# Making k from rows that the first norm has not scaled yet, in a two-block kernel on one core

## The chip, the cores and the metric

The kernel runs on one core of a Trainium2 chip. The time is the device time of one execution in microseconds, and the number given is the median of three executions. All arithmetic is float32.

## The reference, cut to what matters

Two transformer-like blocks are computed on 512 tokens of width 1024, with 16 meta tokens put in front (528 rows in all). The change touches only the start of the first block:

```python
def rmsnorm(x, g):
    ms = mean(x * x, axis=-1)                     # one number for each row (token)
    return x * rsqrt(ms + EPS) * g                # g: one number for each channel
xn = rmsnorm(concat(meta_tokens, x), g_mix_pre)
proj = xn @ w_in                                  # 1024 x 6160
q, k, v, r, a_low, u, z_gla, z_ssm = split(proj)
log_a = log_sigmoid(a_low @ w_gate_up + b_gate) / 16
o = gla_chunked(q, k, v, log_a)                   # causal gated linear attention, chunks of 64
...
```

What follows (the SSM branch, GLU, feed-forward, and the second block with attention, convolution and a mixture of experts) is the same before and after.

The factor rsqrt(ms + EPS) belongs to a token and the product with `w_in` runs over channels, so that (x g s) W = s ((x g) W) for the scale s of each token.

## The kernel before, in words

Everything is kept with channels on the partitions and tokens along the free dimension: x is the tile `x_in` (`HT0`), 8 blocks of 128 channels by 528 tokens. Weights come in 1 MB units of 128x2048 float32 in the order of a list (`PLAN`: k 0 and 1, v 0 to 3, q 0 and 1, u, r and so on). A unit lands in one of three `ring` buffers. ScalarE copies it to a rounded high part (`high`, line 936), VectorE subtracts to get the low part (`low`, lines 1532 to 1536), both into one of two sides of `wsplit`, and TensorE makes three products of each pair (high by high, high by low, low by high; `three`). Unit n can be split only when unit n-2 has been used, and a ring buffer is loaded again when its low part is made.

Each engine has its own function (`tensor`, `scalar`, `vector`, `gpsimd`, `sync`), whose instructions run in the order in which they are written; names in a table stand for semaphore counts (`sig` sets one, `at` waits for one). PSUM's eight banks go round: `fresh` takes the bank that was closed longest ago and waits until its last tenant was read out ("free"). All 8 banks have had the eight `gate` products of line 458 as tenants when unit v 2 starts, so its first bank is free when VectorE has read the first of them at line 1698.

The start of the program, engine by engine:

- SyncE issues the loads of `vecs`, `cst`, x in four pieces, `wal`, `wgu`, three weight units, `bc`.
- ScalarE squares the 8 blocks of x (line 969), TensorE sums the squares over channels with a matrix of ones (lines 418 to 424: 8 products of 512 and 8 of 16 columns), ScalarE takes the root (line 962), VectorE the reciprocal (1548). The result `rstd` (`rst`) holds each token's scale on every partition.
- VectorE makes x g s block by block (1563, 128x528), ScalarE its high part (976), and VectorE (even blocks, 1567) and GpSimd (odd blocks, 2480) the low part. `at("xn", k)` is block k.
- TensorE makes k: unit k 0 block by block as xn comes, four banks at once (`linear` with `each`), 96 products of 264 columns, then unit k 1, 96 more, then the 48 small products of the low gate (`alow`, line 431), then v 0 and v 1, 60 products of 512 columns each, then the `gate` products (458), which need `alow_out` of VectorE (1575), then v 2 and so on.
- ScalarE copies k out of PSUM (950) and takes part in a chain of small operations on SSM parameters.
- VectorE does that chain behind the norm: lines 1657 to 1690, with `next_low` for k 1 (at 1662), v 0 (at 1682) and v 1 (at 1688) between its parts, then four `turns` (1621), `next_low` for v 2, `alow_out`, two `weights_out` (1638), and then the 8 additions of line 1698 that read the gate banks. All of this is in one fixed order.

Of the kernel before, what the change touches and what calls it, by code (L numbers as in the profile page):

```python
# [16 lines left out]
NT = 528  # L17
# [130 lines left out]
def program(nc, W, wmoe, mcst, vecs, cst, xT, wal, wgu, bc, rw, posr, posc, xslot, yslot, prep, bbar, ushuf, yshuf, out):  # L148
    ctx = ExitStack()
    with ctx:  # L150
# [60 lines left out]
        def vec(name):  # L211
            o, n = VOFF[name]
            return vt[:, o:o + n]
# [8 lines left out]
        HT0 = tile("x_in", 0, 8, NT)  # L222
# [40 lines left out]
        rt4 = small[:, 44:48]  # L263
# [93 lines left out]
        def tensor(g):  # L357
# [20 lines left out]
            def linear(name, i, cuts, nk=8, size=2048, each=None, beside=None, after=None):  # L378
# [23 lines left out]
                for j in range(per):  # L402
                    m = slice(128 * j, 128 * j + 128)
                    for tag, xh, xl in cuts:
# [7 lines left out]
                        banks.close(name, per * i + j, tag)  # L412

            halves = [(n, xnh[:, :, lo:hi], xnl[:, :, lo:hi]) for n, (lo, hi) in enumerate(HALVES)]
            xr = [(0, xnh[:, :, 16:NT], xnl[:, :, 16:NT])]

            ba, bb = fresh("ms", 0), fresh("ms", 1)
            p.wait_ge(cst_landed, 16)
            for k in range(8):  # L420
                p.wait_ge(*at("sq", k))
                mm(ba, ones, sq[:, k % 4, 0:512], k == 0, k == 7)
                mm(bb[:, 0:16], ones, sq[:, k % 4, 512:NT], k == 0, k == 7).then_inc(*p.sig(("ms", 0), ("ms", 1), ("summed", k)))
            banks.close("ms", 0)
            banks.close("ms", 1)

            for i in range(2):
                linear("k", i, halves, each="xn")
            for h, (lo, hi) in enumerate(HALVES):  # L430
                b = fresh("alow", h)[0:16, 0:hi - lo]
                p.wait_ge(*at("wal"))
                for k in range(8):
                    t = three(b, walh[:, k, :], wall[:, k, :], xnh[:, k, lo:hi], xnl[:, k, lo:hi], k == 0, k == 7)
                t.then_inc(*p.sig(("alow", h)))
                banks.close("alow", h)
# [492 lines left out]
        def scalar(g):  # L929
# [33 lines left out]

            for k in range(8):
                a.wait_ge(x_landed[k // 2], 16)
                if k > 3:
# [1840 lines left out]
```

## Time and profile before

| | us |
|---|---|
| median of three executions | 1802.95 (1801.0 to 1804.73) |
| the profiled execution | 1801.47 |
| its span in the trace | 1799.6 |
| TensorE busy | 1683.7 (94% of the span) |
| VectorE busy | 1208.6 (67%) |
| ScalarE busy | 748.4 (42%) |
| GpSimd busy | 306.6 (17%) |

The span runs from the first to the last instruction of the trace; the profiled execution's own time is 1.87 us longer. Times inside the trace are counted from the start of the span. A busy TensorE is one that has a matmul under way, not one at its peak. "Idle before" of an instruction is the time that its engine waited, with the instruction that released it.

### The profile page before, as it was taken

How to read it: one execution, taken by the hardware profiler on the slowest of the kernel's cores; microseconds unless marked ns; L12 is line 12 of the kernel's file. 1: busy time of each engine (PE TensorE's matmuls, PEld its weight loads, DVE VectorE, ACT ScalarE, POOL GpSimd, SP SyncE). 2: the span in 40 equal slices, each digit the busy share in tenths (PEclk: the TensorE clock that was granted, in tenths of full speed). 3: DMA queues.
4: the chain of work that ended last, by engine and by line, in shares of the span. 5: the costliest groups of instructions: out<-in, count | busy, mean ns of one | idle time of the engine just before them, and what ended most of it. 6: DMA issues, size and time to landing. Idle time of an engine off the chain costs nothing. (4 is left out here: it accounts for less than half of the span.)

```text
span 1799.6 us, 19630 instructions
## 1 busy us (share of the span) xinstructions
PE 1683.7 (94%) x8110; PEld 1324.5 (74%) x8110; DVE 1208.6 (67%) x1568; ACT 748.4 (42%) x969; POOL 306.6 (17%) x178
## 2 busy tenths in 40 slices
PE   6999899899999989999999989999898997999994
PEld 5778777677888867888887877878544776777773
DVE  5979768863333347733656446959787556999996
ACT  5252454444222333222222224342466136777773
POOL 1000012114000000000000015433200003554540
PEclk9999999899999989999999979999999999999997
DMA  5425222423222313435435412222200205999993
GB/s 233 165 102 180 77 95 67 138 88 129 111 94 94 140 71 140 164 117 210 164 116 187 164 48 77 94 94 94 71 0 1 94 1 201 395 386 390 368 376 146
DMA packets 59642, 264.52 MB, mean 147 GB/s; under 512 B 21648, under 2 KB 22288, under 8 KB 33056
## 3 DMA queue, kind: packets, MB, share of 16 engines
q1 hardware_dynamic: 34896, 159.10, 24.3%
q0 software_dynamic: 15184, 99.90, 14.1%
q10 hardware_dynamic: 9472, 4.26, 0.8%
q8 instruction: 64, 1.05, 0.2%
q14 instruction: 26, 0.21, 0.0%
HBM read 239.80 MB, written 23.44 MB: 146 GB/s over the span
## 5 line engine op out<-in xcount | busy, mean ns | idle before, releaser
L368 PE MATMUL bank<-h_high,wsplit 128*128 128x512 f32 x992 | 325.2, 405 | 11.5 <-ACT norm_tmp L1235 4.9
L1536 DVE TENSOR_TENSOR wsplit<-ring,wsplit 128x2048 fp32r<-128x2048 f32 x75 | 171.8, 2290 | 159.5 <-ACT wsplit L936 159.3
L936 ACT ACTIVATE wsplit<-ring 128x2048 fp32r<-128x2048 f32 x98 | 187.0, 1908 | 208.2 <-PE bank L368 197.0
L368 PEld LDWEIGHTS bank<-h_high,wsplit 128*128 128x128 f32 x992 | 188.8, 190 | 60.0 <-ACT norm_tmp L1235 5.0
L368 PE MATMUL bank<-xn_high,wsplit 128*128 128x512 f32 (+1 forms) x832 | 217.2, 348 | 12.1 <-DVE xn_low L1567 8.0
L368 PE MATMUL bank<-h_low,wsplit 128*128 128x512 f32 x496 | 198.0, 399 | 0.0
L368 PEld LDWEIGHTS bank<-xn_high,wsplit 128*128 128x128 f32 x832 | 145.5, 190 | 34.7 <-DVE xn_low L1567 8.1
L368 PE MATMUL bank<-f_high,wsplit 128*128 128x512 f32 x512 | 168.3, 401 | 0.0
L368 PE MATMUL bank<-xn_low,wsplit 128*128 128x512 f32 (+1 forms) x416 | 143.8, 346 | 0.0
L1536 POOL TENSOR_TENSOR wsplit<-ring,wsplit 128x2048 fp32r<-128x2048 f32 x23 | 106.8, 4643 | 176.5 <-ACT wsplit L936 176.4
L2561 POOL DMA_INDIRECT ring<-in_wmoe,indices x42 | 84.4, 2009 | 192.0 <-DVE routing L2328 131.5
L2528 POOL TENSOR_TENSOR x<-x,z 128x512 f32<-128x512 f32 x8 | 11.1, 1386 | 610.6 <-DVE z L2008 610.6
L368 PEld LDWEIGHTS bank<-f_high,wsplit 128*128 128x128 f32 x512 | 96.3, 188 | 22.0
L368 PEld LDWEIGHTS bank<-h_low,wsplit 128*128 128x128 f32 x496 | 94.6, 191 | 23.4 <-issue 1.8
L368 PE MATMUL bank<-f_low,wsplit 128*128 128x512 f32 x256 | 101.2, 395 | 0.0
L2123 DVE SCALAR_TENSOR_TENSOR bank<-conv_in,vecs,bank 128x512 f32<-128x512 f32 x116 | 87.7, 756 | 4.1
L368 PEld LDWEIGHTS bank<-xn_low,wsplit 128*128 128x128 f32 x416 | 79.0, 190 | 10.7 <-issue 1.0
L368 PE MATMUL bank<-m_high,wsplit 128*128 128x512 f32 x256 | 81.4, 396 | 3.8 <-DVE wsplit L1536 2.9
L368 PE MATMUL bank<-g_high,wsplit 128*128 128x512 f32 x256 | 80.8, 395 | 0.0
L368 PE MATMUL bank<-wsplit,block_high 128*128 128x512 f32 x232 | 75.5, 407 | 5.4 <-DVE block_low L2382 5.4
L1278 ACT ACTIVATE f_high<-norm_tmp 128x512 fp32r<-128x512 f32 x32 | 20.3, 634 | 122.0 <-DVE norm_tmp L2067 122.0
L368 PE MATMUL bank<-parts,block_high 128*128 128x512 f32 x216 | 68.9, 400 | 0.0
(480 smaller groups left out, 3337.3 us busy)
## 6 DMA issues: line engine op xcount, KB each, us to landing
ring<-in_W SPq DMA_DIRECT2D x122, 1024.0 KB, 4.8
weights_out<-prep SPq DMA_DIRECT2D x8, 864.0 KB, 5.6
prep<-weights_out_early POOLq DMA_DIRECT2D x8, 576.0 KB, 3.1
xslot<-zeros SPq DMA_DIRECT2D x7, 516.0 KB, 5.0
yslot<-block_out SPq DMA_DIRECT2D x7, 512.0 KB, 8.9
block<-xslot SPq DMA_DIRECT2D x6, 516.0 KB, 12.1
prep<-turns_early POOLq DMA_DIRECT2D x8, 288.0 KB, 2.4
x_in<-in_xT SPq DMA_DIRECT2D x4, 528.0 KB, 6.5
```

The source lines that it names most:

```text
L368: return g.matmul(o, l, r, start=first, stop=last_, skip_group_check=True)
L936: g.activation(wst[:, side(n), 0, :], ringt[:, n % RING, :], ACT.Copy).then_inc(*a.sig(("high", n)))
L1278: g.activation(fh[:, j % 16, :], nrm[:, 2 * z, :], ACT.Square).then_inc(*a.sig(("f_high", j)))
L1536: g.tensor_tensor(wst[:, side(n), 1, :], ringt[:, n % RING, :], hi, SUB).then_inc(*t.sig(("low", n), ("released", n)))
L2123: g.scalar_tensor_tensor(out=o, in0=i, scalar=cw[:, c, k:k + 1], in1=grown, op0=MUL, op1=ADD).then_inc(*v.sig(("convolved",), ("free", "co ...
L2528: g.tensor_tensor(X[:, k, :], X[:, k, :], Z[:, k, :], ADD).then_inc(*q.sig((name, "x", k)))
L2561: g.indirect_dma_start(slots[c % NS], None, wmoe, indexed(x)).then_inc(slot_landed[c % NS], 16)
```

## The change

The sum of squares is taken by token: ScalarE squares as before, VectorE adds the 8 squared blocks into one tile `square_sum`, and TensorE sums that over channels with five products of one column, so that a token's sum stands on a partition. ScalarE takes the root of 128x4 and 16x1 values, VectorE their reciprocal, and TensorE spreads them over a row again with five small products (`spread_first`), which ScalarE copies into `rst`. Meanwhile k is made of x g without the scale: ScalarE makes the high part `xgh` (x g rounded), VectorE the low part `xgl` from x, g and the high part. When a product of k leaves PSUM, VectorE multiplies it by `rst` (`k_out`, two operations of 128x264 for each of 4 heads), in place of ScalarE's copy. After two heads it makes xn as before, with the other two heads' `k_out` between and behind. The low gate moves from ahead of v to between v 0 and v 1. The split of k 1 and v 0 moves forward. The first weight unit is loaded ahead of x, `cst` behind x. VectorE's chain on SSM parameters waits for GpSimd's last block.

```diff
-            ba, bb = fresh("ms", 0), fresh("ms", 1)
+            linear("k", 0, raw, each="xg")
+            b = fresh("ms")
             p.wait_ge(cst_landed, 16)
-            for k in range(8):
-                p.wait_ge(*at("sq", k))
-                mm(ba, ones, sq[:, k % 4, 0:512], k == 0, k == 7)
-                mm(bb[:, 0:16], ones, sq[:, k % 4, 512:NT], k == 0, k == 7).then_inc(...)
-            for i in range(2):
-                linear("k", i, halves, each="xn")
+            p.wait_ge(*at("square_sum"))
+            for m in range(4):
+                mm(b[:, m:m + 1], sq_sum[:, 16 + 128 * m:144 + 128 * m], ones[:, 0:1], m == 0, False)
+            mm(b[0:16, 4:5], sq_sum[:, 0:16], ones[:, 0:1], False, True).then_inc(*p.sig(("ms",)))
+            def spread_first():
+                p.wait_ge(*at("inverse", "ms"))
+                mm(banks.at("ms")[:, 16:32], rt5[0:16, 4:5].to_broadcast([16, 128]), ident[0:16, 0:16], True, True)
...
+                b = fresh("ms", "scale")
+                for m in range(4):
+                    t = mm(b[:, 128 * m:128 * m + 128], rt5[:, m:m + 1].to_broadcast([128, 128]), ident, True, True)
...
+            linear("k", 1, raw, between=spread_first)
...
+                    p.wait_ge(*at("xn", 4 * kg + 2))
+                    p.wait_ge(*at("xn", 4 * kg + 3))
...
+                    if half == 0 and kg == 0:
+                        p.wait_ge(*at("xn", 6))
+                        p.wait_ge(*at("xn", 7))
+                        low_gate()
```

```diff
 # scalar
+            high(0)
+            a.wait_ge(vecs_landed, 16)
             for k in range(8):
                 a.wait_ge(x_landed[k // 2], 16)
+                g.activation(xgh[:, k, :], HT0[:, k, :], ACT.Copy, scale=vec("g_mix_pre")[:, k:k + 1])
                 if k > 3:
-                    a.wait_ge(*at("summed", k - 4))
+                    a.wait_ge(*at("square_added", k - 4))
                 g.activation(sq[:, k % 4, :], HT0[:, k, :], ACT.Square)
-            high(0)
-            root(("ms", 1), rst[:, 512:NT], 1024, 16)
-            root(("ms", 0), rst[:, 0:512], 1024, 512)
+            root_table()
+            high(1)
+            a.wait_ge(*at("ms"))
+            g.activation(rt5[:, 0:4], banks.at("ms")[:, 0:4], ACT.Sqrt, ...)
+            g.activation(rt5[0:16, 4:5], banks.at("ms")[0:16, 4:5], ACT.Sqrt, ...)
+            next_high("k", 1)
+            a.wait_ge(*at("ms", "meta"))
+            g.activation(rst[:, 0:16], banks.at("ms")[:, 16:32], ACT.Copy)
+            a.wait_ge(*at("ms", "scale"))
+            g.activation(rst[:, 16:NT], banks.at("ms", "scale"), ACT.Copy)
...
-            next_high("k", 0)
-            copies("k", 0, 2, 2, lambda j, c: K[:, j, slice(*HALVES[c])])
-            next_high("k", 1)
-            copies("k", 1, 2, 2, lambda j, c: K[:, j, slice(*HALVES[c])])
```

```diff
 # vector
+            def square_added(k):
+                v.wait_ge(*at("sq", k))
+                v.wait_ge(*v.own())
+                g.tensor_tensor(sq_sum, sq[:, 0, :] if k == 1 else sq_sum, sq[:, k % 4, :], ADD)
+            def k_out(j):
+                for c, (lo, hi) in enumerate(HALVES):
+                    v.wait_ge(*at("k", j, c))
+                    g.tensor_tensor(K[:, j, lo:hi], banks.at("k", j, c)[:, 0:hi - lo], rst[:, lo:hi], MUL)
             low(v, g, 0)
-            inverse(rst[:, 512:NT], "root", "ms", 1)
-            inverse(rst[:, 0:512], "root", "ms", 0)
+            for k in range(8):
+                v.wait_ge(*at("xg_high", k))
+                g.scalar_tensor_tensor(out=xgl[:, k, :], in0=HT0[:, k, :], scalar=vec("g_mix_pre")[:, k:k + 1], in1=xgh[:, k, :], op0=MUL, op1=SUB)
+                if k > 1:
+                    square_added(k - 1)
+            square_added(7)
+            low(v, g, 1)
+            v.wait_ge(*at("root", "ms"))
+            g.reciprocal(rt5[:, 0:4], rt5[:, 0:4])
+            g.reciprocal(rt5[0:16, 4:5], rt5[0:16, 4:5])
+            next_low("k", 1)
+            v.wait_ge(*at("rst"))
+            k_out(0)
+            k_out(1)
             for k in range(9):
...
+                if k == 3:
+                    k_out(2)
+            k_out(3)
...
             v.wait_ge(*at("dt"))
+            v.wait_ge(*at("xn", 7))
...
-            next_low("k", 0)
...
-            next_low("k", 1)
```

```diff
 # sync
             g.dma_start(vt[:, :], vecs)
-            g.dma_start(ct[:, :], cst[:, 0:NCST])
+            load(0)
             for i in range(4):
                 g.dma_start(HT0[:, 2 * i:2 * i + 2, :], xT[:, 2 * i:2 * i + 2, :])
+            g.dma_start(ct[:, :], cst[:, 0:NCST])
             g.dma_start(walt, wal)
             g.dma_start(wgut[0:16, :], wgu)
-            loads(0, RING)
+            loads(1, RING)
```

## Rows read from the trace of the kernel before

**Rows 1.** The page's busy table of the whole span, one line.

```profile
PE 1683.7 (94%) x8110; PEld 1324.5 (74%) x8110; DVE 1208.6 (67%) x1568; ACT 748.4 (42%) x969; POOL 306.6 (17%) x178
```

**Rows 2.** TensorE's timeline, 0 to 112 us: start, duration, what, count, idle before.

```profile
27.03 0.56 PE L368 MATMUL bank<-xn_high,wsplit 128*128 128x264 f32 x1 [8.04 <-DVE xn_low L1567]
...
42.02 0.39 PE L368 MATMUL bank<-xn_high,wsplit 128*128 128x264 f32 x1 [1.49 <-DVE wsplit L1536]
...
59.60 0.63 PE L368 MATMUL bank<-wsplit,xn_high 128*128 128x512 f32 x2
...
87.60 3.82 PE L368 MATMUL bank<-a_low,wgu 16*128 16x264 f32 x16
91.46 0.79 PE L368 MATMUL bank<-wsplit,xn_high 128*128 128x512 f32 x2
```

**Rows 3.** Who waited for whom, 90 to 400 us: total, times, longest.

```profile
PEld bank L368 <- DVE log_a L1698: 0.5, 1, 0.5
```

**Rows 4.** VectorE's timeline, 0 to 112 us.

```profile
24.70 1.45 DVE L1563 SCALAR_TENSOR_TENSOR x_in<-x_in,vecs,rstd 128x528 f32<-128x528 f32 x2
26.18 0.71 DVE L1567 TENSOR_TENSOR xn_low<-x_in,xn_high 128x528 fp32r<-128x528 f32 x1
...
30.53 1.83 DVE L1563 SCALAR_TENSOR_TENSOR x_in<-x_in,vecs,rstd 128x528 f32<-128x528 f32 x1
...
37.87 0.19 DVE L1657 TENSOR_TENSOR ssm_small<-vecs,ssm_small 128x32 f32<-128x32 f32 x1 [0.22 <-ACT ssm_small L980]
...
39.67 2.29 DVE L1536 TENSOR_TENSOR wsplit<-ring,wsplit 128x2048 fp32r<-128x2048 f32 x1
...
42.99 0.19 DVE L1671 TENSOR_TENSOR powers<-ssm_small 128x32 f32<-128x32 f32 x1 [0.70 <-ACT ssm_small L993]
...
51.55 2.28 DVE L1536 TENSOR_TENSOR wsplit<-ring,wsplit 128x2048 fp32r<-128x2048 f32 x1
...
61.84 2.29 DVE L1536 TENSOR_TENSOR wsplit<-ring,wsplit 128x2048 fp32r<-128x2048 f32 x1
...
75.68 0.70 DVE L1632 TENSOR_TENSOR products_early<-phasors,phasors 128x288 f32<-128x288 f32 x1 [1.33 <-DMA prep<-turns_early]
...
81.17 0.75 DVE L1575 COPY a_low<-bank 16x264 f32<-16x264 f32 x2
...
90.92 3.29 DVE L1698 TENSOR_SCALAR log_a<-bank,vecs 128x264 f32<-128x264 f32 x8
...
109.28 2.29 DVE L1536 TENSOR_TENSOR wsplit<-ring,wsplit 128x2048 fp32r<-128x2048 f32 x1 [5.89 <-ACT wsplit L936]
```

**Rows 5.** DMA issues, 0 to 70 us: count, KB each, median us to landing.

```profile
x_in<-in_xT SPq DMA_DIRECT2D x4, 528.0 KB, 6.5
...
cst<-in_cst SPq DMA_DIRECT2D x1, 463.5 KB, 3.5
vecs<-in_vecs SPq DMA_DIRECT2D x1, 210.5 KB, 2.5
```

**Rows 6.** Stretches: length, busy us (count) of PE PEld DVE ACT POOL, PEclk, DMA share, GB/s.

```profile
7.00:10.00 3.00, 3.00 (x5) 1.55 (x6) 0.00 (x0) 2.06 (x4) 0.00 (x0) 1.00 1.04 400
28.00:30.25 2.25, 2.25 (x12) 2.25 (x11) 2.25 (x3) 0.89 (x2) 0.93 (x2) 0.50 0.00 0
```

**Rows 7.** ScalarE's timeline, 0 to 80 us.

```profile
6.20 1.18 ACT L969 ACTIVATE squares<-x_in 128x528 f32<-128x528 f32 x2 [4.16 <-DMA x_in<-in_xT]
...
15.25 1.89 ACT L936 ACTIVATE wsplit<-ring 128x2048 fp32r<-128x2048 f32 x1
...
76.55 0.60 ACT L1004 ACTIVATE v<-bank 128x512 f32<-128x512 f32 x1 [0.81 <-PE bank L368]
```

**Rows 8.** All engines, 661 to 665 us: a norm summed by token.

```profile
661.98 1.02 PE L368 MATMUL bank<-cst,norm_tmp 128*128 128x1 f32 x8 [1.58 <-DVE norm_tmp L1987]
...
663.73 1.13 PE L368 MATMUL bank<-cst,small 128*128 128x128 f32 x8 [0.73 <-DVE small L1992]
```

**Rows 9.** GpSimd's timeline, one of the four subtractions of the first norm.

```profile
30.06 1.74 POOL L2480 TENSOR_TENSOR xn_low<-x_in,xn_high 128x528 fp32r<-128x528 f32 x1 [1.32 <-ACT xn_high L976]
```

More of the change, by code:

```diff
@@ L219, in program @@
         ident, ones, eps = con("ident"), con("ones"), con("eps")
-        HT0 = tile("x_in", 0, 8, NT)
+        HT0, sq_sum = tile("x_in", 29712, 8, NT), tile("square_sum", 26768, NT)
+        xgh, xgl = tile("xg_high", 18320, 8, NT, dt=F32R), tile("xg_low", 22544, 8, NT, dt=F32R)
         walt, wgut = tile("wal", 4224, 8, 16), tile("wgu", 4352, 512)
@@ L376, in weights, with linear @@
                 return [wst[:, side(n), z, 0:size].rearrange("p (k m) -> p k m", k=nk) for z in range(2)]
-            def linear(name, i, cuts, nk=8, size=2048, each=None, beside=None, after=None):
+            def linear(name, i, cuts, nk=8, size=2048, each=None, beside=None, after=None, between=None):
                 n = UNIT[name, i]
@@ L412, in linear @@
                         banks.close(name, per * i + j, tag)
+                        if between and j == 0 and tag == 0:
+                            between()
             halves = [(n, xnh[:, :, lo:hi], xnl[:, :, lo:hi]) for n, (lo, hi) in enumerate(HALVES)]
+            raw = [(n, xgh[:, :, lo:hi], xgl[:, :, lo:hi]) for n, (lo, hi) in enumerate(HALVES)]
             xr = [(0, xnh[:, :, 16:NT], xnl[:, :, 16:NT])]
-            ba, bb = fresh("ms", 0), fresh("ms", 1)
+            linear("k", 0, raw, each="xg")
@@ L437, in tensor, with low_gate @@
+            linear("k", 1, raw, between=spread_first)
+            def low_gate():
+                for h, (lo, hi) in enumerate(HALVES):
+                    b = fresh("alow", h)[0:16, 0:hi - lo]
+                    p.wait_ge(*at("wal"))
+                    for k in range(8):
+                        t = three(b, walh[:, k, :], wall[:, k, :], xnh[:, k, lo:hi], xnl[:, k, lo:hi], k == 0, k == 7)
+                    t.then_inc(*p.sig(("alow", h)))
+                    banks.close("alow", h)
             for half in range(2):
@@ L1552, in scaled @@
                 g.scalar_tensor_tensor(out=o, in0=x, scalar=gain, in1=rs, op0=MUL, op1=MUL).then_inc(*v.sig((name, k)))
+            def square_added(k):
+                v.wait_ge(*at("sq", k))
+                v.wait_ge(*v.own())
+                g.tensor_tensor(sq_sum, sq[:, 0, :] if k == 1 else sq_sum, sq[:, k % 4, :], ADD).then_inc(
+                    *v.sig(*[("square_added", n) for n in ((0, 1) if k == 1 else (k,))], ("square_sum",)))
+            def k_out(j):
+                for c, (lo, hi) in enumerate(HALVES):
+                    v.wait_ge(*at("k", j, c))
+                    g.tensor_tensor(K[:, j, lo:hi], banks.at("k", j, c)[:, 0:hi - lo], rst[:, lo:hi], MUL).then_inc(*v.sig(("free", "k", j, c), ("k_out", j, c)))
             low(v, g, 0)
-            inverse(rst[:, 512:NT], "root", "ms", 1)
-            inverse(rst[:, 0:512], "root", "ms", 0)
             v.wait_ge(vecs_landed, 16)
-            v.wait_ge(*v.own())
+            for k in range(8):
+                v.wait_ge(*at("xg_high", k))
+                g.scalar_tensor_tensor(out=xgl[:, k, :], in0=HT0[:, k, :], scalar=vec("g_mix_pre")[:, k:k + 1], in1=xgh[:, k, :].bitcast(F32),
+                                       op0=MUL, op1=SUB).then_inc(*v.sig(("xg", k)))
+                if k > 1:
[3 more added lines that the diff above has]
+            v.wait_ge(*at("root", "ms"))
+            g.reciprocal(rt5[:, 0:4], rt5[:, 0:4]).then_inc(*v.sig())
+            g.reciprocal(rt5[0:16, 4:5], rt5[0:16, 4:5]).then_inc(*v.sig(("inverse", "ms")))
+            next_low("k", 1)
+            v.wait_ge(*at("rst"))
+            k_out(0)
+            k_out(1)
             for k in range(9):
                 if k < 8:
-                    v.wait_ge(x_landed[k // 2], 16)
                     g.scalar_tensor_tensor(out=HT0[:, k, :], in0=HT0[:, k, :], scalar=vec("g_mix_pre")[:, k:k + 1], in1=rst,
```

27 lines of the change are left out of this document (13 added, 14 removed).

## The prediction

> **What bounds the kernel now.** The page's busy table comes first: TensorE is busy for 94% of the span, VectorE for 67% [rows 1]. That average doesn't price this change, which lies in the first 60 us, so TensorE's timeline comes next, read for its idle times. TensorE sits idle for 8.04 us before k, until the first xn is there, and for 1.49 us before k 1, whose split is late; from 42.02 us it runs without a gap that counts until v 2 starts at 91.46 [rows 2]. The third view is the one that decides here, the list of waits: at v 2 the weight load waited 0.5 us for VectorE's line 1698 [rows 3]. VectorE's timeline says why: line 1698 starts at 90.92, and its first operation, some 0.45 us long, frees the bank that v 2 needs [rows 4]. TensorE's last gate product ended at 87.60 + 3.82 = 91.42 [rows 2]. So at 91.4 us the two engines arrive together. Ahead of that point VectorE is a second chain without slack: it starts with the scale `rst`, ready at 24.6, and runs through xn, the SSM parameters, `turns` and `weights_out` to line 1698. From v 2 on all engines are tied to TensorE (at 109.28 VectorE waited 5.89 us for a split whose side of `wsplit` v 2 had to free [rows 4]), so what is won or lost at v 2 stays to the end. Two sums are needed, one for each engine, and the later one counts.
>
> **TensorE's sum.** Before, `vecs`, `cst` and x 0, 1202 KB, were there by 6.20, when the first square ran [rows 5, 7]; in the changed order `vecs` and the first 1 MB unit are 1234 KB, so the unit lands at about 6.3 at 400 GB/s [rows 6]. The queue issues in order, and x 0 follows 1.3 us later, under the split. High part 1.89 [rows 7], low part 2.29 (as at 39.67 [rows 4]): 10.5. The first `xgl` costs about what a value operation of 128x528 does, 1.45 / 2 = 0.73 [rows 4]: TensorE starts at 11.3 instead of 27.03. I take 13.5 again: 24.8. Does VectorE keep up? A block is one `xgl` and one square added, which waits for its predecessor: 0.73 + 0.71 (as at 26.18 [rows 4]) + about 0.1 of waiting = 1.5; `xgl` 7 is there at 20.3, the last sum at 21.9, the low part of k 1 at 24.2. It does, with 0.6 to spare. ScalarE's two operations a block cost 1.2 (6.20 [rows 7]), less than VectorE's. The 16 old products of the sum (TensorE was otherwise idle) go for nothing.
>
> Five products of one column at 1.02 / 4 each are 1.3 [rows 8], to 26.1; the first group of k 1, 24 x 0.122 = 2.9, to 29.0; five spreading products at 1.13 / 4, 1.4 [rows 8], to 30.4; the other 72 of k 1, to 39.2, against 53.7 before. Root and reciprocal lie beside k 1. TensorE alone would be 14.5 us ahead.
>
> **VectorE's sum, up to xn.** `rst` comes after the spreading, 30.4, plus ScalarE's copy of a bank, 0.60 [rows 7]: 31.0. The split of v 0 (ScalarE from about 26.6, VectorE to 30.8) is just covered by that; if it weren't, VectorE would be late by the same amount. Then `k_out` of two heads, four operations reading PSUM at 3.29 / 8 = 0.41 each [rows 4]: 1.65. The first xn value starts at 32.7; before it started at 24.70 [rows 4]. **8.0 us later**: the reciprocal of 512 columns has gone, but sums, a whole unit k 0, the first group of k 1 and the spreading now stand in front.
>
> **Behind it.** The xn loop is as before but for `k_out` of head 2. It falls beside GpSimd's subtraction (1.74 us at 30.06 [rows 9]). A VectorE operation with two inputs in SBUF took 1.83 beside that, against 0.73 alone [rows 4]: it was held until GpSimd had done. If `k_out`, with one input in PSUM, isn't held, it uses up that dead time in part, and the two values behind it end 0.7 later than before; if it is held, 1.7. I take 0.7, since the row shows the hold only for two SBUF inputs. `k_out` of head 3 and the low part of `wal` lie in the wait for ScalarE's exponential ahead of 37.87 and for GpSimd's last block: nothing (at most 0.8). The Trainium skill, page SBUF — State Buffer, section Who interferes with whom, says that a VectorE instruction with at most one SBUF input, outside the 2-port modes, doesn't contend with GpSimd. By that rule the sum is the one taken here, with a hold as in the row it would be 1.0 more; no row here shows such a pair.
>
> Two splits leave the chain. The one at 51.55 gives its whole 2.3 back. The one at 39.67 covered a round trip through ScalarE (a table, sine, absolute value), ready at about 41.9 anyway; what goes is mainly the idle 0.70 at 42.99, where the sine stood behind four copies of k. I take 0.75; the ends are 0 and 2.3.
>
> **Sum at line 1698**: 8.0 + 0.7 - 0.75 - 2.3 = 5.65, so VectorE gets there at 96.6 instead of 90.92, and v 2 starts at 97.1 instead of 91.46.
>
> **Where TensorE's lead goes.** v 0 waits for GpSimd's third block of xn (31.80 + 8.0 = 39.8) and runs 14.0, half of 59.60 to 87.6, to 53.8; the low gate, 48 products, to 59.7. v 1 needs its low part, which VectorE starts at 61.84 + 5.65 and ends at 69.8: an idle stretch of **10 us**, and some 1.6 at the lower clock behind it. v 1 ends at 85.4, `a_low` (81.92 before) comes at 87.6, the gate products end at 91.4, and TensorE waits again, 5 to 6 us, for line 1698. The 14.5 us of lead are three waits.
>
> Sum: +5.65 us, on the profiled execution's own 1801.47: 1807.1. The median of the runs, 1802.95, is 1.5 above that execution; from it the sum gives 1808.6. I forecast 1808.0, between them. About 0.2% (3.6 us) is what a measurement of this kernel can tell from no change.
>
> **The rivals.**
> 1. *Two or three terms of VectorE's chain are at their low ends*, and the result is within 0.2%. k 0 without the lower clock: -0.6 (then the split of k 1 binds at 24.2). The split at 39.67 gives 2.3: -1.55. The wait of 1.33 on a store at 75.68 [rows 4] vanishes: -1.3. Together +2.2, 1805.1 from the median; any two leave +2.8 to +3.8. For it: each is a bound that no row excludes. Against: they must meet, and the store's wait is tied to VectorE's own pace. Chance 0.25.
> 2. *TensorE's lead survives* (the other side). Place: line 1698. VectorE would have to be there before 90.92, that is, `rst` and `k_out` over by 27.0 rather than 32.7. From there each us is a us won, at most the 14.5 of TensorE's sum, 1788.5; half of that, 1795.7, is the price I put on it. For it: the cold start of TensorE and both its idle times do go. Against: the order on VectorE is fixed, and the last square alone is added at 21.9. Chance 0.11.
> 3. *Slower still*: the start is not what the sum has. If the first unit shared the bandwidth with x instead of landing first, it would come with the last of x's 2112 KB, 5.4 us later at 400 GB/s, and everything with it: 1813.4. If TensorE kept the lower clock for all of k 0 (its operands come no faster than it uses them), 23.4 instead of 13.5: +9.9, 1817.9. Against the first: `vecs`, `cst` and x 0 had the whole rate for themselves (1202 KB by 6.20) with x 1 to x 3 queued behind. Against the second: before, at the same density of products, the lower clock cost k 0 only 1.8. Chance 0.06.
> 4. *The change doesn't do what it says*: the sum of squares by token is only used after k 0, so if k 1 waited for `rst`, TensorE would lose some 2 us; that lies in the forecast's range and gets no chance of its own.
>
> **How the numbers follow.** Forecast 0.58, and with rival 3 slower by over 0.2%: 0.64. Rival 1: 0.25. Rival 2: 0.11. Range: the low ends give +2.2 on 1801.47, 1803.7, less 1.2 for a `k_out` that costs nothing (0.7) and the spread of executions, 1802.5; on the other side the lower clock for twice as long (+1.8), the held `k_out` (+1.0) and an `xgl` slower than the value operation by 0.15 a block (+1.1): 1808.6 + 3.9 = 1812.5. Rival 2 and most of rival 3 lie outside.
>
> **What would show it.** TensorE starts k at 11 to 12; k 1 ends near 39. First xn value at 32 to 33. A wait of TensorE of 8 to 12 us for VectorE's split ahead of v 1, near 60 to 70. Line 1698 at 96 to 97, v 2 at 97, and the same distance at every later stage, with the idle time of 5.89 ahead of the split of q 0 still there. If line 1698 starts before 91 the forecast is wrong, whatever k did; if TensorE doesn't wait ahead of v 1, VectorE's chain is shorter than I have it, and the first xn value says by which term.

## The result, and the profile after

The changed kernel takes 1809.4 us, the median of 20 executions (1802.73 to 1811.65); the kernel before took 1804.87, the median of 20 executions on the same chip (1799.94 to 1810.29). The ratio is 1.0023, with a 95% interval of 1.0014 to 1.0032: 4.2 us slower, with 2.5 and 5.8 us at the ends. The forecast was 1808.0. The profiled execution took 1809.3 us, and its trace spans 1807.5.

The page's busy table answers to [rows 1]: nothing in it tells the two kernels apart.

```profile
PE 1682.5 (93%) x8098; PEld 1326.6 (73%) x8098; DVE 1218.1 (67%) x1591; ACT 750.7 (42%) x972; POOL 311.5 (17%) x178
```

TensorE's timeline answers to [rows 2] (start, duration, what, count, idle before). The waits of 8.04 us ahead of k and of 1.49 us ahead of k 1 are gone, and behind 60 us, where there was none, there are three: 10.20, 0.92 and 5.67 us.

```profile
11.34 0.56 PE L369 MATMUL bank<-xg_high,wsplit 128*128 128x264 f32 x1 [11.34 <-DVE xg_low L1599]
...
24.83 1.08 PE L369 MATMUL bank<-cst,square_sum 128*128 128x1 f32 x10
...
28.95 1.48 PE L369 MATMUL bank<-cst,small 16*128 16x16 f32 x10
...
39.33 0.70 PE L369 MATMUL bank<-wsplit,xn_high 128*128 128x512 f32 x2
...
69.50 1.22 PE L369 MATMUL bank<-wsplit,xn_high 128*128 128x512 f32 x2 [10.20 <-DVE wsplit L1565]
...
86.29 3.82 PE L369 MATMUL bank<-a_low,wgu 16*128 16x264 f32 x16 [0.92 <-DVE a_low L1629]
...
95.78 1.22 PE L369 MATMUL bank<-wsplit,xn_high 128*128 128x512 f32 x2 [5.67 <-DVE log_a L1751]
```

TensorE starts k 15.7 us sooner and starts v 0 at 39.33 instead of 59.60 (which was behind the low gate then), and it is late at v 2 all the same: 95.78 instead of 91.46, +4.32. The list of waits, 90 to 400 us, says for whom: the row that stood at 0.5 us [rows 3] is now at 6.1. Line 1751 here is line 1698 of before.

```profile
PEld bank L369 <- DVE log_a L1751: 6.1, 1, 6.1
PE bank L369 <- DVE log_a L1751: 5.7, 1, 5.7
```

VectorE's timeline answers to [rows 4]:

```profile
26.38 0.18 DVE L1606 RECIPROCAL small<-small 128x4 f32<-128x4 f32 x1 [2.96 <-ACT small L1004]
...
28.18 2.29 DVE L1565 TENSOR_TENSOR wsplit<-ring,wsplit 128x2048 fp32r<-128x2048 f32 x1 [1.59 <-ACT wsplit L959]
31.09 1.45 DVE L1593 TENSOR_TENSOR k<-bank,rstd 128x264 f32<-128x264 f32 x4 [0.62 <-ACT rstd L1009]
32.46 1.44 DVE L1614 SCALAR_TENSOR_TENSOR x_in<-x_in,vecs,rstd 128x528 f32<-128x528 f32 x2
...
37.63 0.76 DVE L1593 TENSOR_TENSOR k<-bank,rstd 128x264 f32<-128x264 f32 x2
...
46.06 0.19 DVE L1712 TENSOR_TENSOR ssm_small<-vecs,ssm_small 128x32 f32<-128x32 f32 x1 [0.21 <-ACT ssm_small L1016]
...
50.51 0.19 DVE L1725 TENSOR_TENSOR powers<-ssm_small 128x32 f32<-128x32 f32 x1
...
67.16 2.29 DVE L1565 TENSOR_TENSOR wsplit<-ring,wsplit 128x2048 fp32r<-128x2048 f32 x1
...
76.53 2.50 DVE L1686 TENSOR_TENSOR products_early<-phasors,phasors 128x288 f32<-128x288 f32 x4 [0.37 <-DMA prep<-turns_early]
...
85.48 0.75 DVE L1629 COPY a_low<-bank 16x264 f32<-16x264 f32 x2
...
95.24 3.29 DVE L1751 TENSOR_SCALAR log_a<-bank,vecs 128x264 f32<-128x264 f32 x8
...
114.19 2.29 DVE L1565 TENSOR_TENSOR wsplit<-ring,wsplit 128x2048 fp32r<-128x2048 f32 x1 [6.48 <-ACT wsplit L959]
```

Read the rows as differences to their partners in [rows 4]. The first xn value is 7.76 us later (24.70 to 32.46), the first SSM operation 8.19 (37.87 to 46.06), line 1725 7.52 (42.99 to 50.51), the split of v 1 5.32 (61.84 to 67.16), the gate additions 4.32 (90.92 to 95.24), and the split of q 0, for which VectorE waits as it did before, 4.91 (109.28 to 114.19). So the chain starts almost 8 us late, gets half of it back, and what is left at 95 us is not won back: the first operation that writes `h`, behind the first block, starts at 1082.9 against 1077.1, +5.8.

A second profile of each kernel (f3 and e8 below) shows how far one pair can be trusted. The gate additions stand at 95.98 and 91.10, +4.88; v 2 at 96.52 and 91.95, +4.57; `h` at 1084.6 and 1076.2, +8.4. From `h` to the end of the trace the kernel before took 722.5 and 721.9, and the kernel of e4, which is the same there, 727.6. Up to v 2 two profiles of one kernel agree within 1 us. At q 1 they are 1.7 us apart in the kernel before (133.78 and 135.50) and 1.25 in the changed one (138.77 and 140.02), and the second profile of before falls 3.8 us behind the first by 286 us and is 0.9 ahead of it at 459. So the theories are tested at v 2, and the medians of many executions carry the total.

The pair shows one more link, which the prediction had no term for. Unit k 0 took 13.5 us in the first profile of each kernel and 14.5 (before) and 14.4 (changed) in the second; the slow products at its start lasted longer. In the kernel before that is made up out of the wait ahead of k 1 (1.49 and 0.44 us). In the changed kernel the sum of squares stands behind k 0, so `k_out` found `rst` ready 0.8 us later (31.91 instead of 31.09), and v 2 started 0.7 later. Three variants with the same start fit: k 0 of 13.8, 14.2 and 14.5 us, `rst` ready for 31.27, 31.80 and 31.91 (e1, e2, f2).

### The profile page after: what moved, and what is told of

The parts are those of the page before. It is cut to its first block and busy times, and to the rows that moved or that the text cites. A ratio compares the mean times of both kernels' runs of the same rounds, so it can differ in the third digit from the quotient of the medians.

```text
span 1807.5 us, 19635 instructions
## 1 busy us (share of the span) xinstructions
PE 1682.5 (93%) x8098; PEld 1326.6 (73%) x8098; DVE 1218.1 (67%) x1591; ACT 750.7 (42%) x972; POOL 311.5 (17%) x178
## 5 line engine op out<-in xcount | busy, mean ns | idle before, releaser
L369 PE MATMUL bank<-xn_high,wsplit 128*128 128x512 f32 (+1 forms) x704 | 192.3, 359 | 2.6 <-DVE wsplit L1565 1.5
L369 PEld LDWEIGHTS bank<-xn_high,wsplit 128*128 128x128 f32 x704 | 124.5, 189 | 25.1 <-DVE wsplit L1565 2.0
L369 PE MATMUL bank<-xn_low,wsplit 128*128 128x512 f32 (+1 forms) x352 | 125.0, 355 | 0.0
L369 PEld LDWEIGHTS bank<-xn_low,wsplit 128*128 128x128 f32 x352 | 66.2, 188 | 11.1 <-issue 1.4
```

The lines of the kernel that those rows point to most:

```text
L369: return g.matmul(o, l, r, start=first, stop=last_, skip_group_check=True)
```

## The experiments

The theory: VectorE's fixed order from `rst` to line 1751 sets v 2; TensorE's lead is spent in waits that cost nothing. The distances that tell it apart are 1 to 10 us at v 2, where two profiles of one kernel differ by 0.5 and 0.7. e1 to e4, f2, f3 and e8 are one execution each. Their times differ by little more than executions of one kernel do (1799.94 to 1810.29 for the kernel before), so the stages carry what is said of them.

**e1: is the 10 us wait ahead of v 1 the loss?** The changed kernel with the split of v 1 ahead of the SSM chain.

```diff
 # vector                              # scalar: next_high("v", 0) likewise,
+            next_low("v", 0)          #         ahead of dt's exponential
             v.wait_ge(*at("dt"))
...
             phasors(EA)
-            next_low("v", 0)
```

> The changed kernel, with the split of v 1 moved ahead of VectorE's SSM chain (same instructions, other order). Theory (VectorE's chain up to the gate additions sets the start of v 2): TensorE's wait of 10.2 us ahead of v 1 goes, v 1 starts near 59 instead of 69.5, but the wait only moves: 12 to 14 us ahead of the gate products instead of 0.9, gate additions at 95.2 to 95.8, v 2 at 95.8 to 96.4, and the stage of the first norm by token after the GLU (reciprocal of 128x4, 669.0 in the changed kernel, 663.4 before) within 1 us of 669.0. Rival (the idle stretch of 10 us and the lower clock behind it are the loss): v 2 near 85 and that reciprocal near 659.

1809.24 us, beside 1803.15 for the kernel before. TensorE's timeline:

```profile
85.92 7.40 PE L369 MATMUL bank<-a_low,wgu 16*128 16x264 f32 x16 [12.52 <-DVE a_low L1629]
...
95.41 1.22 PE L369 MATMUL bank<-wsplit,xn_high 128*128 128x512 f32 x2 [2.08 <-DVE log_a L1751]
...
138.77 0.50 PE L369 MATMUL bank<-xn_high,wsplit 128*128 128x512 f32 x1 [1.51 <-DVE wsplit L1565]
```

The wait ahead of v 1 is gone and has moved whole to the gate products (12.52), v 2 starts at 95.41 instead of 95.78, and q 1 at 138.77, as in the changed kernel (140.02 in its second profile). Those 10 us of idle time cost nothing. The gate products took 7.40 instead of 3.82 us behind the longer wait (granted clock 0.50, the lower level of 1.2 GHz), and that too was taken from a wait (5.67 to 2.08).

**e2 and e3: does the place of the gate additions set v 2?** The two `weights_out` ahead of them (8.9 us, 86.34 to 95.24) are moved behind them, in the changed kernel and in the kernel before.

```diff
             alow_out()
-            weights_out(0)
-            weights_out(1)
             for h in range(4):
...                                    # the 8 gate additions
             next_low("v", 2)
+            weights_out(0)
+            weights_out(1)
             v.wait_ge(*v.own())
             weights_out(2)
```

> The changed kernel, with weights_out 0 and 1 (8.9 us of VectorE) moved behind the gate additions and the split of v 3. Theory: the gate additions now wait for the gate products themselves, v 2 starts at 90.1 to 90.5 instead of 95.78 (5.4 earlier), the split of q 0 starts near 109 instead of 114.2, the reciprocal at 669.0 moves to 663.5 to 664.5, the time to that of the kernel before or 1 us less. Rival (the loss is elsewhere: the PE clock, the loads): less than 2 us of change.

> The same move in the kernel before. Theory: TensorE and VectorE reach v 2 together there, so freeing VectorE alone gives nothing: v 2 at 91.4 to 91.5, the reciprocal at 663.4 within 1 us either way. Rival (VectorE alone bounds that stage in both kernels): v 2 several us earlier.

e2: 1807.34 us. TensorE's timeline, and VectorE's gate additions:

```profile
90.76 0.73 PE L369 MATMUL bank<-wsplit,xn_high 128*128 128x512 f32 x2
...
135.97 0.54 PE L369 MATMUL bank<-xn_high,wsplit 128*128 128x512 f32 x1 [4.35 <-DVE wsplit L1565]
```

```profile
88.26 3.61 DVE L1749 TENSOR_SCALAR log_a<-bank,vecs 128x264 f32<-128x264 f32 x8 [1.31 <-ACT exp_gate L1042]
...
111.46 2.28 DVE L1565 TENSOR_TENSOR wsplit<-ring,wsplit 128x2048 fp32r<-128x2048 f32 x1
```

v 2 moved from 95.78 to 90.76 without a wait, as the theory has it. But only 2.8 us of these 5.0 are left at q 1 (138.77 to 135.97), which now waits 4.35 us for its split. The moved work stands ahead of the split of q 0 instead: it fills the 6.48 us that VectorE waited there, and 2.3 us more, so that this split starts at 111.46 and not 5.0 us ahead of 114.19. That second part I had not expected: behind v 2 VectorE has little room.

e3: 1812.35 us, against 1803.15. VectorE waits 9.74 us ahead of the additions, since in this kernel the gate products come at 90.37 (87.60 before; the start of k is 1.2 us late in this execution, and k 1 took 1.5 longer) and not sooner:

```profile
91.63 3.61 DVE L1696 TENSOR_SCALAR log_a<-bank,vecs 128x264 f32<-128x264 f32 x8 [9.74 <-ACT exp_gate L1010]
```

v 2 stayed with the gate products, as expected, at 94.12: 2.7 us late, all of it lost ahead of the edit. But q 1 starts at 139.32 after a wait of 5.94, 5.5 us late. The other 2.9 us are the edit's, and they are the loss of e2 again: the split of q 0 starts at 114.82 without a wait, where VectorE had 5.89 to spare. That loss I had left out. By the stages, the same move gains 2.8 us where TensorE has a lead and costs 2.9 where it has none; each is one execution, and at q 1 two profiles of one kernel lie 1.3 to 1.7 apart.

**e4: are TensorE's idle times before k 1 worth anything to the kernel before?** The split of k 1 right behind that of k 0:

```diff
             low(v, g, 0)
+            low(v, g, 1)
...
-            next_low("k", 0)
```

> The kernel before with one part of the change alone: the split of k 1 made right behind that of k 0, ahead of the root. Theory: TensorE's idle 1.49 us ahead of k 1 goes, k starts some 0.6 later (the reciprocal waits for the split), v 0 starts some 0.9 earlier (58.7); VectorE's chain loses 0.75 and gains 0.6, so the gate additions stay at 90.8 and v 2 at 91.3 to 91.5: no change of the time. Rival (TensorE's idle time in front of k is what counts): v 2 0.9 to 1.5 earlier.

1806.7 us. The wait of 1.49 is gone, gate additions at 90.72, v 2 at 91.36, q 1 at 133.69 (before 133.78), `h` at 1077.3 (before 1077.1). No gain at any stage up to there, but it is not the test that I had meant: v 0 was to start at 58.7 and started at 59.61, as before (59.60), because k started 0.95 us later and its two units took 25.85 us instead of 25.30 without the wait. TensorE was never early. Against the first profile of the kernel before, this execution falls back by 3.8 us between 1372 and 1389 us, in stages that the edit doesn't touch.

**e5 and e6: is it the length of VectorE's chain?** The first part of the SSM chain (angle, sine, lambda, the powers) needs only `vecs`. It is put into VectorE's idle times at the start: in the changed kernel 8.2 us ahead of its first split and 4.5 around the reciprocal, in the kernel before some 18. For this `squares` and `x_in` are laid elsewhere in memory, and the small products have a tile of their own.

```diff
 # vector                                          # scalar: Exp, Sin, Abs and Sin of
+            ssm_a()          # angle              # these parameters likewise
             low(v, g, 0)
...
+                if k == 0:
+                    ssm_b()  # cosine's argument
...
             low(v, g, 1)
+            ssm_c()          # lambda, powers
             v.wait_ge(*at("root", "ms"))
...
-            v.wait_ge(*at("dt"))
             v.wait_ge(*at("xn", 7))
-            g.tensor_tensor(mag, ar, dt_, MUL)
...
-            phasors(PW)
             unit(EA[:, 1])
```

> The changed kernel, with the first part of VectorE's SSM chain (angle, lambda, the powers) moved from behind the first norm into VectorE's idle time: the angle ahead of the first split, the powers between the split of k 1 and the root. Theory: VectorE's chain up to the gate additions is 8.3 us shorter, TensorE's lead becomes worth something: wait ahead of v 1 down from 10.2 to about 2 us, gate additions at 86 to 88 instead of 95.2, v 2 at 87 to 88.5 instead of 95.78, and all later stages 7 to 8.5 us earlier (the reciprocal of 128x4 at 661 to 662 instead of 669.0). Time 7 to 8 us under the changed kernel, 3 to 4 under the kernel before. Rival (the lead isn't worth anything because a later stage bounds both): v 2 earlier, but q 1 and everything behind it less than 3 us earlier.

> The same move in the kernel before (angle and powers ahead of the first norm, in VectorE's idle start). Theory: VectorE has 6.7 us to spare at the gate additions, but TensorE is the bound there, having started k at 27: v 2 comes only 1.5 us earlier (the idle 1.49 ahead of k 1 goes, since its split no longer stands behind the angle), 89.9 to 91.5. Time 0 to 1.5 us under the kernel before. Rival (VectorE's chain alone sets the time in both kernels): 5 us or more.

e5: 1799.46 us, the median of 12 executions (1792.97 to 1806.98), ratio to the kernel before 0.9982 (0.9965 to 0.9999). Against the changed kernel that is 7 us less by the two ratios (0.9982 and 1.0023) and 9 by the medians, each taken against its own kernel before (the ends of the two intervals allow 3 to 12), from an edit that takes no work out. The time is unsteady: six executions lie between 1793.0 and 1797.4 and six between 1801.5 and 1807.0, and the profiled one is the fastest. VectorE, then TensorE:

```profile
86.79 3.28 DVE L1765 TENSOR_SCALAR log_a<-bank,vecs 128x264 f32<-128x264 f32 x8
```

```profile
61.11 0.73 PE L369 MATMUL bank<-wsplit,xn_high 128*128 128x512 f32 x2 [1.87 <-DVE wsplit L1565]
...
77.84 5.32 PE L369 MATMUL bank<-a_low,wgu 16*128 16x264 f32 x16 [2.51 <-DVE a_low L1703]
...
87.33 1.22 PE L369 MATMUL bank<-wsplit,xn_high 128*128 128x512 f32 x2 [4.17 <-DVE log_a L1765]
```

The chain is 8.45 us shorter at the additions (95.24 to 86.79), and v 2 follows by the same 8.45: 95.78 to 87.33. The wait ahead of v 1 falls from 10.20 to 1.87. The reciprocal that [rows 8] stand around was expected at 661 to 662 and came at 656.3, 12.7 us sooner than in the changed kernel: 4 us more than v 2 gained, most of it between 190 and 450 us, where profiles of one kernel differ by as much. I don't put these 4 us down to the edit.

e6: the same edit in the kernel before: 1804.6 us, the median of 12, ratio 1.0002 (0.9989 to 1.0016). VectorE, then TensorE:

```profile
88.72 3.18 DVE L1713 TENSOR_SCALAR log_a<-bank,vecs 128x264 f32<-128x264 f32 x7 [1.04 <-ACT exp_gate L1012]
```

```profile
87.47 4.27 PE L368 MATMUL bank<-a_low,wgu 16*128 16x264 f32 x16
91.67 1.22 PE L368 MATMUL bank<-wsplit,xn_high 128*128 128x512 f32 x2
```

v 2 starts at 91.67, with VectorE's additions at 88.72 waiting for the gates. There TensorE was the other chain without slack, so a shorter VectorE chain bought nothing. I had given it up to 1.5 us for the wait ahead of k 1, which fell to 0.39; but k 0 took 0.9 us longer in this execution, and v 0 started at 59.47, as before. This pair is the case for the theory: one edit, worth 8.45 us at v 2 and 7 to 9 in the time where TensorE is ahead, and nothing at v 2 or in the time where it isn't.

**e7: what is the change worth with an order made for it?** e5, with VectorE's order set by when each result is wanted.

```diff
             unit(EB[:, 1])
+            next_low("v", 0)           # split of v 1
             phasors(EB)
...
             phasors(EA)
-            next_low("v", 0)
-            for cb in range(4):
-                turns(cb)
-            next_low("v", 1)
             alow_out()
-            weights_out(0)
-            weights_out(1)
+            turns(0)
+            next_low("v", 1)
+            turns(1)
             for h in range(4):         # the 8 gate additions
...
+            turns(2)
             next_low("v", 2)
+            turns(3)
             v.wait_ge(*v.own())
-            weights_out(2)
+            weights_out(0)
+            weights_out(1)
...                                     # turns 6, 7 and weights_out 2 later still;
                                        # scalar's next_high("v", 0) and the stores follow
```

> The kernel of the run e5, with VectorE's order behind the first norm made for TensorE's new dates: split of v 1 inside the SSM chain, the low gate's copy and the gate additions ahead of most turns and all weights_out, first decay ahead of the last two turns. Theory: TensorE no longer waits ahead of v 1, gates near 73.5, v 2 at 77 to 79 instead of 95.78; then VectorE's sum of work bounds: q 1 starts 12 to 19 us earlier than in the changed kernel (120 to 127 instead of 138.8), part of that given back in the attention heads, and at the reciprocal of 128x4 the lead is 9 to 12 us (657 to 660 instead of 669.0). Time 9 to 12 us under the changed kernel. Rival (VectorE's work only moves, so the gain ends at that of e5): 661 to 662.

1795.65 us, the median of 6 executions (1790.68 to 1797.74), ratio to the kernel before 0.9944 (0.9926 to 0.9962): under both kernels, and 0.8% under the changed one (13 us by the medians, each against its own kernel before, and 14 by the ratios; 9 to 12 were expected). TensorE ran from 11.57 to 130 us without a wait (its gate products at 74.32, v 2 at 78.08, 13.4 us ahead of the kernel before, and q 0 at 107.62, 13.4 ahead of 121.02). Then it gives back more than half: at 147.84 the lead over the kernel before is 11.3 us (159.09 there), at 154.17 8.4 (162.53), and at the reciprocal that [rows 8] stand around 5.8 (657.6 to 663.4). The first long waits of TensorE are these:

```profile
132.20 0.39 PE L369 MATMUL bank<-xn_high,wsplit 128*128 128x264 f32 x1 [2.13 <-DVE wsplit L1565]
...
154.17 0.56 PE L369 MATMUL bank<-xn_high,wsplit 128*128 128x264 f32 x1 [3.72 <-DVE gla_scores L1871]
```

Where the first part of the lead goes shows in the stretch 100 to 165 us (length, then busy us and count of PE, PEld, DVE, ACT, POOL; granted clock; DMA), first in e7, then in e5:

```profile
100.00:165.00 65.00, 58.43 (x332) 50.13 (x331) 62.33 (x100) 20.03 (x27) 5.81 (x10) 0.95 0.45 157
```

```profile
100.00:165.00 65.00, 61.92 (x350) 50.86 (x349) 54.27 (x88) 22.75 (x28) 5.26 (x9) 1.00 0.43 143
```

VectorE is busy for 62.33 of 65 us (96%) and TensorE waits for it. There VectorE's amount of work is the limit, and the change raised it (by the page from 1208.6 us in 1568 operations [rows 1] to 1218.8 in 1591).

That the new order beats e5 rests on the times alone (ratios 0.9944 and 0.9982, whose intervals don't touch). In the profiles e7's lead over e5 is 9.3 us at v 2, 6.9 at 147.84, 2.6 at 168 and 0.1 at 268, and at the reciprocal e5's execution, the fastest of its twelve, is 1.3 us ahead. The rival on record for e7, that the work only moves and the gain ends at that of e5, isn't excluded by them. What e7's further edits would do in the kernel before was not run.

**f1: what if the norm comes first and k stays unscaled?** This turns back the largest term, the 8 us. x is loaded ahead of the first weight unit, the sum and the spreading stand ahead of k 0, and `k_out` and the split of v 0 go behind the xn loop.

```diff
 # tensor
-            linear("k", 0, raw, each="xg")
             b = fresh("ms")
...
-            linear("k", 1, raw, between=spread_first)
+            spread_first()
+            linear("k", 0, raw, each="xg")
+            linear("k", 1, raw)
 # vector
-            low(v, g, 0)               # now behind square_added(7)
...
-            next_low("k", 1)           # split of v 0, now behind k_out(3)
             v.wait_ge(*at("rst"))
-            k_out(0)                   # k_out 0, 1: now behind the xn loop
-            k_out(1)
...
             phasors(PW)
+            k_out(2)
+            k_out(3)
+            next_low("k", 1)
```

> The changed kernel with the norm ahead of k: x is loaded ahead of the first weight unit, the squares are summed and spread before k 0, so rst is ready about 8 us earlier, and the xn values start without waiting for any product of k; k_out moves behind the xn loop (heads 0, 1) and behind the powers (heads 2, 3), the split of v 0 into VectorE's chain. TensorE gives up its early start of k (22 to 23 us instead of 11.3). Theory (the time at which rst is ready sets VectorE's chain, and that chain sets v 2; TensorE's early start is worth nothing): last square added at 18 to 19, first xn value at 23 to 24.5 instead of 32.46, less the split of v 0 that the chain now holds (2.3) and with k_out unchanged in number: gate additions at 89 to 91 instead of 95.24, no wait of TensorE ahead of v 1 over 2 us, v 2 at 89.5 to 91.5 instead of 95.78; 1802 to 1805, 4 to 7 us under the changed kernel and within 2 of the kernel before. Rival (TensorE's early start of k is what keeps the changed kernel from being slower still): v 2 is late by what k starts later, 11 us, less the wait ahead of v 1: 97 or more, and the kernel is at 1810 or above.

1807.57 us, the median of 10 executions, ratio to the kernel before 1.0014 (0.9997 to 1.0031); by its time it can't be told from either kernel. VectorE, then TensorE:

```profile
25.26 1.45 DVE L1612 SCALAR_TENSOR_TENSOR x_in<-x_in,vecs,rstd 128x528 f32<-128x528 f32 x2 [1.14 <-ACT rstd L1009]
...
49.88 0.43 DVE L1594 TENSOR_TENSOR k<-bank,rstd 128x264 f32<-128x264 f32 x1 [2.01 <-PE bank L369]
50.23 2.28 DVE L1566 TENSOR_TENSOR wsplit<-ring,wsplit 128x2048 fp32r<-128x2048 f32 x1
...
93.90 3.29 DVE L1751 TENSOR_SCALAR log_a<-bank,vecs 128x264 f32<-128x264 f32 x8
```

```profile
21.98 2.61 PE L369 MATMUL bank<-cst,small 16*128 16x16 f32 x10 [0.74 <-DVE small L1607]
...
52.57 1.21 PE L369 MATMUL bank<-wsplit,xn_high 128*128 128x512 f32 x2 [2.72 <-DVE wsplit L1566]
...
94.44 1.22 PE L369 MATMUL bank<-wsplit,xn_high 128*128 128x512 f32 x2 [2.60 <-DVE log_a L1751]
```

Both answers missed. The rival (v 2 at 97 or later) falls: v 2 came sooner, at 94.44. Of the theory the first half holds: the first xn value is 7.20 us sooner (32.46 to 25.26), and the first SSM operation with it, 7.30 (46.06 to 38.76). But of that only 1.34 is left at the additions (95.24 to 93.90), where I had 4 to 6. I had written that TensorE's early start of k is worth nothing, and that is wrong: it is what lets the split of v 0 be done while VectorE waits for `rst` anyway, and what has the products of k ready when `k_out` comes. With k late, VectorE waits 2.01 us in mid-chain for the last product of k 1, and the split of v 0 (2.28) and the late `k_out` of heads 2 and 3 (1.5) stand in the chain: 5.8 of the 7.3 us. The norm's small products, now the first work of an idle TensorE, took 2.61 us instead of 1.48, and so delayed `rst` by another us; the first xn value was expected at 24.5 at the latest.

**f2: is `k_out` held beside GpSimd?** The changed kernel with `k_out` of heads 0, 1 and 2 behind low parts in the xn loop, where GpSimd's subtractions run, and none ahead of the loop.

```diff
-            k_out(0)
-            k_out(1)
             for k in range(9):
...
-                if k == 3:
-                    k_out(2)
+                if k % 2 and k < 7:
+                    k_out(k // 2)
```

> The changed kernel with k_out of heads 0, 1 and 2 each right behind a low part of xn in the loop, where GpSimd's subtraction runs beside it, instead of heads 0 and 1 ahead of the loop. Theory (an operation with one input in PSUM isn't held beside GpSimd and fills time that the next two-input operation would have waited anyway): first xn value at 31.1 instead of 32.46; each pair lengthens the loop by 0.3 to 0.5 us where it stands beside a subtraction, instead of 1.45 for two pairs ahead of the loop, so the SSM chain starts 0.3 to 1.0 us sooner than at 46.06, and the gate additions likewise sooner than 95.24. Rival (it is held): each pair costs 1.4 or more in the loop and the SSM chain starts at 47 or later. The time itself can't tell these apart, the timeline can.

1808.27 us. VectorE's timeline:

```profile
31.91 1.45 DVE L1612 SCALAR_TENSOR_TENSOR x_in<-x_in,vecs,rstd 128x528 f32<-128x528 f32 x2 [0.64 <-ACT rstd L1009]
...
34.02 0.76 DVE L1593 TENSOR_TENSOR k<-bank,rstd 128x264 f32<-128x264 f32 x2
34.70 1.99 DVE L1612 SCALAR_TENSOR_TENSOR x_in<-x_in,vecs,rstd 128x528 f32<-128x528 f32 x2
36.72 0.71 DVE L1616 TENSOR_TENSOR xn_low<-x_in,xn_high 128x528 fp32r<-128x528 f32 x1
...
94.94 3.29 DVE L1749 TENSOR_SCALAR log_a<-bank,vecs 128x264 f32<-128x264 f32 x8
```

A pair of `k_out` beside GpSimd takes 0.76 us as it does anywhere, and the two values behind it 1.99 instead of 2.53: the pair costs the loop 0.25 us (34.02 to 36.72, 2.70 us, against 2.45 without one). It isn't held. From the moment at which `rst` was there to the first SSM operation it took 13.9 us (31.91 to 45.82) instead of 15.0 (31.09 to 46.06), and the additions stand at 94.94, against 95.98 in f3, whose `rst` came at the same time. Against the first profile of the changed kernel, which the expectation went by, the first SSM operation is only 0.24 us sooner, since `rst` came 0.8 late here.

**f3 and e8: the two kernels again.**

> The changed kernel once more, unchanged, for a second profile: gate additions at 95 to 96.5, v 2 at 95.5 to 97, wait ahead of v 1 of 9.5 to 10.5 us; 1803 to 1811. Shows how much of the distances between single profiles is the spread of executions.

> The kernel before once more, for a second profile. In the two other kernels built on it the first square started at 7.8 to 8.1 us, in its own profile at 6.20; kernels that load the first weight unit ahead of x started k at 11.2 to 11.3 each time. Theory: the first loads' arrival varies by 1 to 2 us, and 1 us of that reaches the scale; so v 2 at 91.5 to 92.7 here, and the changed kernel's 95.78 stands 3.1 to 4.3 behind. Rival: 6.20 and 91.46 again.

f3: 1811.89 us, wait ahead of v 1 of 10.18, additions at 95.98, v 2 at 96.52. e8: 1799.88 us. Its x landed 1.3 us later than in the first profile of before (first square at 7.51 instead of 6.20 [rows 7]), and yet the first xn value is at 24.92, 0.22 later: TensorE's old sum of squares ran in 10.92 us instead of 12.00.

## Why the prediction was right

The forecast was 1808.0, of a kernel that took 1809.4, and the likeliest case came true by its own mechanism: TensorE starts early, VectorE's chain starts late, and the later chain sets v 2. By its own steps:

- *TensorE's sum* held to a tenth: k at 11.34 (11.3), the end of k 0 at 24.8 (24.8), the spreading from 28.95 (29.0), `rst` copied by 31.06 (31.0). Part of that is luck: in the second profile k 0 took 0.9 longer, and these steps came 0.8 later (f3). The 13.5 us of k 0 were read from one execution, and the range had the longer slow start only as a bound.
- *8.0 us later* was 7.76. The difference is `k_out`: four at 1.37 from 31.09 to 32.46, not 1.65, because the 0.41 each came from the row of another operation: the gate additions are 0.40 apart, `k_out` 0.34.
- *0.7 for `k_out` in the loop* was 0.43 (7.76 to 8.19), and f2 prices a pair by itself at 0.25. The row of before showed a hold for two inputs in SBUF only, and I took the pair as not held; f2 shows that. By the rule of the Trainium skill that the prediction cites (SBUF — State Buffer, Who interferes with whom) this was to be, and these runs agree.
- *-0.75 for the split at 39.67* was -0.67 (8.19 to 7.52), and *-2.3 for the one at 51.55* was -2.20 (7.52 to 5.32).
- *The wait of 1.33 on a store* was taken to stay. It went, and a wait of 0.37 one turn earlier came in its place, -0.96 together. It was named among the low ends, with its row; the argument against it, that it is tied to VectorE's own pace, didn't hold: with the same work between, the waits on a store ahead of the additions were 1.33 and 1.30 in the kernel before, 0.37 and 0.35 in the changed one and 0.80 in f1. What sets it was not looked into. This is the largest term that was mis-sized.
- *The sum*: 7.76 + 0.43 - 0.67 - 2.20 - 0.96 = 4.36, measured 4.32 at the additions and at v 2, predicted 5.65. The executions say 4.2 by the ratio.
- *What is won or lost at v 2 stays to the end* held for the change as far as the profiles can tell (+4.3 at v 2, +5.0 at q 1, +5.8 at `h`). It is no rule: where an edit moves VectorE's work behind v 2, part is lost again (e2: 5.0 to 2.8; e7: 13.4 to 5.8).
- *Where the lead goes*: the waits were forecast as 10, 2.2 and 5 to 6 and came as 10.20, 0.92 and 5.67.

That the forecast of 1808.0 came nearer than its sum is partly luck: the shift was 1.4 less than the sum, and the executions of the kernel before ran 1.9 us above the median from which I started (1804.87 and 1802.95).

Rival 1 (within 0.2%) had its mechanism in part: of its three terms one came true, the store's wait, with 0.96 of its 1.3. Its 3.6 us lie inside the interval of the shift (2.5 to 5.8), so "slower by over 0.2%" rests on the middle of that interval. Rival 2 needed VectorE at its additions before 90.92; e5 brought it to 86.79 by another edit, and each of those us was then won, as the rival had it. Rival 3's lower clock for all of k 0 didn't come: k 0 took 13.5 to 14.5 us in the profiles. That the shift is VectorE's chain is shown (e1, e2, e5, e6); that the start of that chain is the whole of it isn't: f1 moved the start by 7.2 and the end by 1.3.

Open is why the late stages differ by more than v 2 does in both pairs of profiles (`h` +5.8 and +8.4, v 2 +4.3 and +4.6). The distance from v 2 to `h` varied from 981 to 988 us without a pattern that I could tie to an edit; in e2, e3 and e7, which move work behind v 2, it was 990 to 993.

## What to carry to other kernels

Two engines that arrive together are two chains: price a change on both, and let the later one decide; the lead of the other turns into waits whose size says nothing of what they cost (e1). Here a head start for one engine paid only when the other's fixed order was made anew for it: the same change was 4 us slower than the kernel before in the old order and 8 us or more faster in a new one (e7), while the part of the new order that is e5's edit gave the old kernel nothing (e6). Work moved behind the meeting point can cost there again, so look for the next one (e2, e3). And an early result is worth what else it lets be done in idle time, so ask that before calling a lead useless (f1).

## What the runs showed of the hardware

- At the start of the program the granted clock reads full while the products run at half rate. In the changed kernel the stretch 11.40 to 14.40 reads 1.00:

```profile
11.40:14.40 3.00, 3.00 (x14) 3.00 (x15) 2.93 (x5) 3.00 (x6) 0.00 (x0) 1.00 1.06 417
...
69.50:73.00 3.50, 3.50 (x8) 2.81 (x9) 3.43 (x7) 0.00 (x0) 0.00 (x0) 0.50 0.68 234
```

  14 products in 3.00 us are 0.21 us each, against 0.122 at full rate. Behind the wait ahead of v 1 the record does read 0.50, the lower level of 1.2 GHz, and there the first products of 512 columns take 0.43 us from start to start. In e7 the slow part of k 0 lasted until 17.4 us. The first microseconds should be judged by the distance of the products, not by the clock's row.
- GpSimd's subtraction is shorter too when VectorE works on PSUM beside it: 1.32 to 1.34 us in all four of f2, which have `k_out` beside them, and 1.73 to 1.83 in the three of the kernel before that run beside values of xn. GpSimd's timeline of the changed kernel, the first row beside values of xn, the second beside `k_out`:

```profile
34.67 1.85 POOL L2533 TENSOR_TENSOR xn_low<-x_in,xn_high 128x528 fp32r<-128x528 f32 x1 [34.22 <-ACT xn_high L1012]
37.84 1.34 POOL L2533 TENSOR_TENSOR xn_low<-x_in,xn_high 128x528 fp32r<-128x528 f32 x1 [1.32 <-ACT xn_high L1012]
```

- The first transfer lands at different times from one execution to the next: the first square of the kernel before and of its two variants with the same loads ran at 6.20, 7.51, 7.81 and 8.06 us. In e8 1.1 of the 1.3 us were made up by the time of the first xn value.
